# Decode keys of a hybrid decoder step: turned by VectorE in 32 by 32 blocks, and loaded by two queues

## The reference, cut to what matters

```python
def dsa_sample(q, k, v, qi, ki, wi, cache_k, cache_v, cache_kidx, page_table, layer):
    ...
    scores = indexer_scores(qi, wi, ki_all, qpos, kpos)
    _, sel = lax.top_k(scores, topk)                   # 256 of 2056 keys for each new token
    valid = sel <= qpos[None, :, None]
    ...
    kg = jnp.where(from_past, cache_k[phys, layer, off], gather(k, n_sel))
    vg = jnp.where(from_past, cache_v[phys, layer, off], gather(v, n_sel))
    return attend_selected(q, kg, vg, valid)

def attend_selected(q, kg, vg, valid):
    logits = jnp.einsum('bthd,btkhd->bhtk', q, kg) * (B_DH ** -0.5)
    logits = jnp.where(valid[:, None], logits, -jnp.inf)
    p = jax.nn.softmax(logits, axis=-1)
    return jnp.einsum('bhtk,btkhd->bthd', p, vg)
```

## Time and profile before

| | us |
|---|---|
| median of three runs | 754.49 |
| profiled execution | 759.38 |
| span of its instructions | 757.7 |
| PE busy | 717.0 (95% of the span) |
| DVE busy | 464.5 (61%) |
| ACT busy | 245.0 (32%) |
| GpSimd busy | 202.2 (27%) |
| share of PE in the chain that ended last | 85% |

### The profile page before, as it was taken

How to read it: one execution, slowest core, us unless ns; L and a number is a source line. 1 busy time by engine, 2 the same in 40 slices (tenths; PEclk the granted TensorE clock), 3 DMA queues, 4 the chain that set the end, 5 groups by cost and what they waited for, 6 DMA issues and landing times.

```text
span 757.7 us, 13976 instructions
## 1 busy us (share of the span) xinstructions
PE 717.0 (95%) x4842; PEld 413.8 (55%) x4842; DVE 464.5 (61%) x976; ACT 245.0 (32%) x559; POOL 202.2 (27%) x329
## 2 busy tenths in 40 slices
PE   4987999999999999999999999999999999879994
PEld 3534444444544555677665556777456677754441
DVE  0204279999999865554556555554747676674435
ACT  3203720114667422222222323222743335430000
POOL 1550005015798722222222222222000002650000
PEclk9989999999999999999999999999999999989998
DMA  9930052042130088898887889886200007400611
GB/s 228 293 109 1 2 204 104 34 146 83 62 113 1 29 266 254 284 351 275 262 277 259 254 255 329 294 270 185 82 1 2 1 2 279 112 15 24 198 42 42
DMA packets 60949, 114.12 MB, mean 151 GB/s; under 512 B 8241, under 2 KB 21634, under 8 KB 60882
## 3 DMA queue, kind: packets, MB, share of 16 engines
q1 hardware_dynamic: 29890, 50.37, 21.1%
q0 software_dynamic: 12512, 40.34, 16.2%
q10 hardware_dynamic: 18480, 22.55, 9.1%
HBM read 106.01 MB, written 7.23 MB: 149 GB/s over the span
## 4 chain that ended last, share of the span: by engine, by line
PE 85%; DVE 3%; DMA 3%; ACT 2%; issue 2%; another core or an unknown queue 2%; ACTq 1%; POOL 1%; SPq 0%; DVEq 0%; POOLq 0%
PE banks L547 16%; PE banks L807 12%; PE banks L793 8%; PE banks L721 7%; PE banks L1072 7%; PE banks L769 4%; PE banks L738 4%; PE banks L895 3%; PE banks L882 3%; PE banks L913 2%; PE banks L685 2%; PE banks L758 2%; PE banks L631 2%; DMA arena<-in_x_prompt 2%
## 5 line engine op out<-in xcount | busy, mean ns | idle before, releaser
L547 PE MATMUL banks<-wbuf,xT 128*128 128x512 f32 (+1 forms) x448 | 150.1, 531 | 3.4 <-issue 3.4
L336 POOL DMA_DIRECT2D arena<-in_cache_v x128 | 68.9, 539 | 198.7 <-issue 198.7
L547 PEld LDWEIGHTS banks<-wbuf,xT 128*128 128x128 f32 (+1 forms) x448 | 66.8, 175 | 80.8 <-issue 74.9
L807 PE MATMUL banks<-wbuf,xT 128*128 128x512 f32 (+1 forms) x288 | 105.0, 530 | 0.0
L1526 DVE TENSOR_REDUCE small<-banks 128x1 f32<-128x512 f32 x32 | 22.1, 691 | 93.0 <-PE banks L738 93.0
L1507 DVE MAX8 small<-arena 64x8 f32<-64x2112 f32 x32 | 75.2, 2348 | 1.3
L1509 DVE MATCH_REPLACE8 arena<-small,arena 64x2112 f32<-64x2112 f32 x32 | 74.7, 2334 | 0.0
L721 PE MATMUL banks<-ident,arena 128*128 128x128 f32 x512 | 68.1, 276 | 0.2 <-DMA arena<-in_cache_k 0.2
L721 PEld LDWEIGHTS banks<-ident,arena 128*128 128x128 f32 x512 | 56.4, 141 | 21.6 <-issue 19.8
L793 PE MATMUL banks<-xT,arena 128*128 128x288 f32 x256 | 67.4, 406 | 0.0
L1270 ACT COPY wbuf<-banks 128x512 f32<-128x512 f32 x64 | 37.2, 582 | 70.0 <-PE banks L721 70.0
(11 more groups left out here) (250 smaller groups left out, 1031.0 us busy)
## 6 DMA issues: line engine op xcount, KB each, us to landing
arena<-in_cache_k SPq DMA_DIRECT2D x128, 256.0 KB, 3.4
arena<-in_cache_v POOLq DMA_DIRECT2D x128, 256.0 KB, 3.9
wbuf<-in_w_in ACTq DMA_DIRECT2D x8, 2048.0 KB, 11.3
arena<-in_w_in ACTq DMA_DIRECT2D x8, 512.0 KB, 6.3
arena<-in_x_prompt SPq DMA_DIRECT2D x4, 512.0 KB, 4.7
wbuf<-in_w_out SPq DMA_DIRECT2D x1, 2048.0 KB, 8.0
xT<-in_w_out SPq DMA_DIRECT2D x1, 2048.0 KB, 13.1
out<-wbuf SPq DMA_DIRECT2D x1, 2048.0 KB, 9.4
```

Of the source, the lines that this page charges most:

```text
L336: e.dma_start(buf[n % 2][:, i, :], cache[bass.ds(pg, 1), 0].rearrange("a p h d -> p (a h d)")).then_inc(arrived[n % 2], 16)
L547: mm = pe.matmul(psum[a * NS:a * NS + ROWS[t], n % PB, 0:w // split], xT[:, c, t * P:t * P + ROWS[t]], wbuf[:, WB[g], c, a * w // split:(a ...
L807: mm = pe.matmul(psum[a * NS:a * NS + ROWS[t], bank, 0:512 // split], xT[:, c, t * P:t * P + ROWS[t]], wbuf[:, WB[g], c, a * 512 // split: ...
```

## The change

In words:

- A page's keys are loaded so that turning 32x32 blocks is enough. Each page is read by 4 DMAs instead of one (`key_pages`): DMA a takes heads 2a and 2a+1 of all 128 keys (pieces of 512 bytes) to the 32 partitions 32a to 32a+31, where partition c holds keys c, 32+c, 64+c and 96+c. DVE's block transpose of [128 x 1024] (two for a group, `turn_keys` on the vector engine) then puts feature d mod 32 of a head on the partitions, in 4 bands of 32 partitions for 4 pairs of heads. PE's 16 turns and the 4 copies from PSUM are gone.
- Groups 0 and 1 are loaded by SP alone. From group 2 on, SP loads pages 0 and 1 and ACT pages 2 and 3 of a group, ACT at the end of its iteration n for group n+2, once DVE has turned the keys of group n (`act.wait_ge(kg_ok, 2 * (n + 1))`).
- The logits lie as [128 x 256]: rows 0 to 63 are the first 256 keys, rows 64 to 127 the other 256, with 8 heads by 8 queries on the 64 rows. They are 8 products of 256 columns instead of 4 of 512, and 2 bias products of 256 columns instead of one of 512. Maximum, exponential, turn and copy of the probabilities are half as wide; the copy (`probs_out`) moves from DVE to ACT. The values are 8 products of 256 columns instead of 16 of 128.
- Since the two halves of the keys lie on different rows, maximum and sum of a sequence are exchanged between the two halves by small copies (`across`). The sequence's output is turned and added up by a product with a constant matrix (`turn_out`, `sel`), and copied to `oT` by ACT (`decoded_out`); the 8 turns and the 4 products of `decode_gate` near the end of the kernel become one DVE product.
- The decode queries and new keys are moved into the new layout by 16 small DMAs and DVE block transposes; the turn of the decode queries and new keys on PE goes; the clearing of the query block moves to GpSimd; ACT copies all four turned prompt-query tiles (before: two, DVE the other two); the gate of group B and half of `w_out` are laid out in another head order.

The diff, cut to its core:

```diff
+        def key_pages(e, n, which):
+            for i in which:
+                pg = e.value_load(pages[0:1, 4 * n + i:4 * n + i + 1], min_val=0, max_val=NPAGES - 1)
+                for a in range(4):
+                    e.dma_start(k_buf[n % 2][32 * a:32 * a + 32, i, :].rearrange("c (t f) -> c t f", t=4),
+                                cache_k[bass.ds(pg, 1), 0].rearrange("z (t c) (a h) d -> a c t (z h d)", t=4, a=4)[a]
+                                ).then_inc(k_in[n % 2], 16)
...
-                for n in range(NG):
-                    if n >= 2:
-                        sp.wait_ge(kg_tr, 4 * (n - 1))
-                    page_loads(sp, cache_k, k_buf, k_in, n)
+                key_pages(sp, 0, range(4))
+                key_pages(sp, 1, range(4))
+                sp.wait_ge(roped, ROPED_Q[NT])
+                for dst, src in ((qst, q_tok), (kst, k_tok)):
+                    for t in range(2):
+                        for a in range(4):
+                            sp.dma_start(dst[32 * a:32 * a + 32, t * P:(t + 1) * P],
+                                         src[32 * t:32 * t + 32, NT, a * P:(a + 1) * P]).then_inc(new_in, 16)
+                for n in range(2, NG):
+                    sp.wait_ge(kg_ok, 2 * (n - 1))
+                    key_pages(sp, n, range(2))
...
                 def logits(n):
                     s, g = n // 4, n % 4
-                    pe.wait_ge(kg_dve, 2 * n + 2)
-                    pe.wait_ge(kg_act, 2 * n + 2)
+                    bank = scores_at(n)
                     if n >= 2:
                         pe.wait_ge(ex, q_no(n - 2) + 1)
-                    bank = psum[:, SB0 + n % 2, :]
-                    pe.matmul(bank, pick[:, s * P:(s + 1) * P], bias_s[:, g * 512:(g + 1) * 512], start=True, stop=False,
-                              skip_group_check=True)
-                    for j in range(4):
-                        mm = pe.matmul(bank[32 * j:32 * j + 32, :], queries(s, j), kg[n % 2][:, j, :],
-                                       start=False, stop=(j == 3), skip_group_check=True)
+                    for half in range(2):
+                        pe.matmul(bank[NS * half:NS * half + NS], pick[:, s * NS:(s + 1) * NS],
+                                  bias_s[:, g * 512 + 256 * half:g * 512 + 256 * half + 256], start=True, stop=False,
+                                  skip_group_check=True)
+                    pe.wait_ge(kg_ok, 2 * n + 2)
+                    for e in range(2):
+                        for k in range(4):
+                            half, b = k // 2, 2 * (k % 2) + e
+                            mm = pe.matmul(bank[32 * k:32 * k + 32], qbd_v[:, s, b, :],
+                                           kgv[n % 2][:, 8 * half:8 * half + 8, b, :], start=False, stop=(e == 1),
+                                           skip_group_check=True)
                     mm.then_inc(qk, 1)
...
+                def turn_out(s):
+                    pe.wait_ge(o_ok, s + 1)
+                    for b in range(2):
+                        mm = pe.matmul(psum[:, MB, M_T][:, 32 * b:32 * b + 32], osb[s % 2][:, b * P:(b + 1) * P],
+                                       sel[:, 32 * b:32 * b + 32], start=True, stop=True, skip_group_check=True)
+                    mm.then_inc(o_tr, 1)
...
                 for n in range(NG + 1):          # TensorE
                     if not last:
-                        turn_keys(n, 0)
                         unit(n, 0)
...
                     if not last:
-                        turn_keys(n, 1)
                         unit(n, 1)
...
                 for n in range(NG + 1):          # ScalarE
                     if n:
                         exponential(n - 1)
                     if n and n % 4 == 0:
                         exponential_new(n // 4 - 1)
+                    if n >= 7 and n % 4 == 3:
+                        decoded_out(n // 4 - 1)
+                    if n:
+                        probs_out(n - 1)
+                    if n and n % 4 == 0:
+                        probs_new_out(n // 4 - 1)
                     if n < NG:
-                        keys_out(n, 1)
-                        keys_out(n, 3)
                         kind, i, h = UNITS[n]
...
+                    if n + 2 < NG:
+                        act.wait_ge(kg_ok, 2 * (n + 1))
+                        key_pages(act, n + 2, range(2, 4))
...
-                def keys_out(n, j):
-                    dve.wait_ge(kg_tr, 4 * n + j + 1)
-                    if j == 0 and n >= 2:
-                        dve.wait_ge(qk, q_no(n - 2) + 1)
-                    nc.vector.tensor_copy(kg[n % 2][:, j, :], psum[:, KB0, :]).then_inc(kg_dve, 1)
+                def turn_keys(n, half):
+                    if half == 0:
+                        dve.wait_ge(k_in[n % 2], 256 * (n // 2) + 256)
+                        if n >= 2:
+                            dve.wait_ge(qk, q_no(n - 2) + 1)
+                    w = slice(1024 * half, 1024 * half + 1024)
+                    nc.vector.transpose(kg[n % 2][:, w], k_buf[n % 2].rearrange("p g n -> p (g n)")[:, w]).then_inc(kg_ok, 1)
...
                     if more:                     # VectorE
-                        keys_out(n, 0)
+                        turn_keys(n, 0)
+                        turn_keys(n, 1)
...
-                    if n:
-                        probs_out(n - 1)
```

335 lines of the change are left out of this document (184 added, 151 removed).

## The result

The changed kernel took 776.59 us (median of 4 runs, 773.7 to 782.38), the kernel before 753.57 beside it: 1.033 of before, 95% interval 1.025 to 1.042. On another chip the same pair gave 1.031 (1.024 to 1.037). I had forecast 741, faster. The profiled execution after has a span of 776.4 us against 757.7.

What follows compares the result with a forecast made beforehand. PE bounded the kernel before; afterwards a cycle through ACT's DMA issues would. Feature groups -0.4, last two -4.2, token groups -9.9, 64-row tiles +1.6, turns behind the loop -0.9: -13.8 from 754.5 gives 741 us, range 704 to 790.

Steps and rivals of the forecast that it cites:

- PE's loss: Decode loop: key turns and half the turn of the probabilities leave PE, 2.11 us a group, 67 us in all.
- DVE's transposes: Decode loop: two block transposes of 1024 columns a group on DVE, taken as 1.285 us each, not on the path.
- ACT's ring: Decode loop: ACT's eight key DMA issues, exponential and PE's work form a cycle, 8.68 us a feature group; chance 50%.
- The bytes: Decode loop's key, value and weight transfers: 7.1 us a feature group, 6.2 a token group, taken as hidden.
- The rival of slow key DMAs: Decode loop: 64 KB key DMAs into 32 partitions make transfers bound, deciding at 205 GB/s; 778 to 808 us; chance 22%.
- estimate of some 815: Decode loop keys at 138 GB/s, the skill's rate for a lone 64 KB load: some 815 us, not made the forecast.
- The rule that I cited: Trainium skill: spreading DMAs over issuing engines brings no bandwidth, only issue time; it changed none of the forecast's terms.
- ACT's queue filling up: Rival in the decode loop: outstanding weight and key DMAs stall ACT's queue 6 us in 6 groups, 777 us; chance 9%.
- The clock: Sign of a wrong forecast: a clock below full inside the decode loop would lengthen every PE term; no size given.

## Why the prediction was wrong

**PE's loss: right.** With whole pages the exponentials follow each other after 6.5 us in many feature groups and 6.1 in many token groups; forecast were 6.60 and 6.15. But even there the gain is some 36 us and not 67. The transfers are full or nearly so (share 1.04 at 315 GB/s in 512-byte pieces, 0.93 in long rows), and with rows of 2 KB the two groups behind the issue of a 2 MB weight load took 15.6 and 15.8 us.

**DVE's transposes: right.** 1.22 us, taken as 1.285.

**ACT's ring: right as a sum, by two errors.** With the bytes cut, 8.07 and 9.37 us, a mean of 8.72 against 8.68; over all 14 feature groups of that run with issues the mean is 8.84. The issue was 0.67 + 4.26 + 0.11 = 5.04 us and not 5.55; a weight load cost 1.30 a time and not 0.37, as the first page number behind it came late too. The last two groups took 6.3 and 6.5, forecast 6.6. That kernel stands at 0.985 of before; the forecast of 741 is 0.982. That the two errors cancelled is luck.

**The bytes: this is the step that failed.** "Keys and weights at 295 and values at 391 ... so the bytes are hidden." In the loop neither rate held. From the queue rows a group needs 1.05 x 82 + 1.05 x 61 = 150 us of an engine, 9.4 us on 16 at a share of 1.0 and 8.4 at the 1.12 that the records reach, where the prediction had 6.2; and the weights come on top. With them the stretch closes: it holds 16.27 / 1.05 = 15.5 groups, 9.0 us each, and 1.12 x 2240 / 15.5 = 162 us of an engine a group, which is 9.0 us again. The engines are never idle there, so the transfers are the period. The 295 GB/s came from a single wide DMA, and for wide DMAs it was near (1.06 x 16 / 295 is 57 us for one MB; whole pages had 60); carrying it over by piece size to DMAs of 32 partitions was wrong, and so was leaving the values at 391.

The rival of slow key DMAs (778 to 808) came near, 1 us above the measured 776.6, but in part by luck. Keys at 82 us for one MB are 195 GB/s on 16 engines, hardly below the 205 from which it decides; with values at 391 that gives a feature group 8.95 us, 0.3 above the ring. It left the values at 391 GB/s and had no large loads. As an estimate from this case's rows: 150 us of keys and values and 15 of weights, on 16 engines at 1.12, are 9.2 us a feature group and 8.4 a token group, by the prediction's own sums some 760 us. The 13.3 us of the groups behind the large loads come on top: 773, close to the 776.6 measured. It too gave the small pieces a part that they don't have in wide DMAs. Its estimate of some 815 from the 138 GB/s is also mis-added: the same sum gives 824.

**A term left out.** The sum of the bytes has no 2 MB weight loads, though two of them are issued in the loop. The groups behind them lost 13.3 of the loop's 24.8 us; with a quarter of the key bytes these groups took 9.0 us each. No run changes these loads alone, so how much is theirs and how much is the narrow DMAs' beside them stays open.

**Ring and bytes together: not shown.** Take away three quarters of the key bytes and 4.8% go; split the ring's issues and about 1% goes, while the waits pass from ACT to the keys. It may be that each late landing also delays the ring and so the next loads. But in the stretch of the windows the transfers explain the period without it, and the split gained about as much with the bytes cut (1.4%) as with all of them.

**The rule that was missed.** The rule that I cited, no bandwidth from more issuing engines, held: 254 GB/s from two queues. The one that spoke against this change stands elsewhere and I did not weigh it. The Trainium skill ("SBUF — State Buffer", Door 1: The DMA port swizzle) says that a DMA's rate goes by how many of 16 ports its partitions reach, that 32 partitions reach 8, and gives 189 GB/s for them at 1 MiB. This case agrees in direction: narrowing contiguous DMAs of 64 KB took the kernel from 1.000 to 1.019 of before, and the full engines moved 254 and 255 GB/s with narrow keys against 315 with whole pages. Its figure is not confirmed: the keys' 82 us for one MB are 195 GB/s, but the same DMAs cost 63 us, 254 GB/s, beside a quarter of the values. An estimate with the page's 189 GB/s for the keys would have been 9.1 us for a feature group and 8.2 for a token group, and by the prediction's own sums some 757 us: no gain, in place of 741.

**ACT's queue filling up: seen, small.** Single issues of 4.98 us stand beside the 2 MB load; the longest idle time before an exponential, 11.6 us, is there.

**The clock: a cost that was only named.** It was 0.93 in the loop (262 to 540 us), where it had been full. After a wait of 2.33 us PE's eight matmuls of a feature unit took 3.30 us, at a granted clock of 0.61, between the levels of 1.2 and 2.4 GHz and nearer the lower; a unit 9.5 us later took 2.11 at 1.00:

```profile
384.33 0.44 PE L803 MATMUL banks<-ident,arena 128*128 128x128 f32 x2 [2.33 <-ACT arena L1336]
384.61 3.30 PE L849 MATMUL banks<-xT,arena 128*128 128x288 f32 x8
...
394.07 2.11 PE L849 MATMUL banks<-xT,arena 128*128 128x288 f32 x8
```

How much of the 18.7 us the clock makes was not isolated by a run. Open as well is by what way DMAs into 32 partitions make the values dearer, what part the pieces 2 KB apart have in the keys' 82 us, and why the order on ACT's queue helps by some 1.5%: neither a strict division of the partitions nor alternate halves did more.

## What to carry to other kernels

When a change cuts loads into more DMAs, price three things apart: the issues on each queue (with what is queued behind them), the bytes, and the partitions that each DMA covers. Count every load of the stretch, the large and rare ones too. Take a transfer rate only from a row with the same partitions and the same company; here neither piece size nor total bytes told it. If two limits come out within 10% of each other, a small error in either decides which one holds.

## What the runs showed of the hardware

- 512-byte pieces cost nothing measurable in DMAs of whole pages over 128 partitions: 0.955 against 0.953 with rows of 2 KB, 315 GB/s in both.
- With key DMAs into 32 partitions the values beside them, unchanged, cost 54 to 61 us of an engine for one MB, against 45 to 49 beside key DMAs into 128 partitions. The keys themselves cost 82 us in 512-byte pieces 2 KB apart, 67 in rows of 2 KB and 58 in wide DMAs of the same size.
- The same narrow DMAs cost 63 us for one MB beside a quarter of the value bytes, and landed after 2.5 us instead of 5.1.
- Behind the issue of a 2 MB load, with the engines full, a group of the loop took 13.4 to 17.8 us where the kernel before had 8.56.
- A source with two strides over the partitions made each issue 0.61 us on SP and 1.02 on ACT (medians), against 0.32 and 0.34, and the kernel 29% longer.
- A block transpose of 128x1024 float32 on DVE took 1.22 us; a copy of 128x512 out of PSUM had taken 0.68.
